# Reordering the attention part of the even layer, and swapping the roles of state and vectors in the sample delta rule

## The chip, the cores and the metric

The kernel runs on one core of a Trainium2 chip. TensorE (PE in the views; its weight loads are PEld) multiplies, VectorE (DVE) and ScalarE (ACT) work on SBUF and PSUM, GpSimd (POOL) does small work and starts some DMAs, SyncE (SP) starts the weight DMAs. The metric is the device time of one execution in microseconds. The kernel before took 1756.63 us as the median of three executions (1753.97 to 1757.15). Its profiled execution took 1756.62 us, of which 1754.9 us are the span from the first to the last instruction.

## The reference

Two trunk layers are run once, for a prompt of 256 tokens and for 8 sample sequences of one token each, D = 1024, all in float32. What the change touches is this, cut to what is computed:

```python
# layer 0, sample side of the differential attention (4 heads, two 64-wide halves, 256 past keys in two pages)
s1 = einsum(q1, k_all[..., :64]) * scale;  s2 = einsum(q2, k_all[..., 64:]) * scale
p  = softmax(s1) - lam * softmax(s2)
o  = p @ v_all
# layer 0, prompt side: the same with a causal mask over 256 keys, query blocks of 128
# layer 1, sample side of the gated delta rule, one token, per sequence b (8) and head h (8), S is 128 x 128
v_new = beta * (v - exp(g) * (k^T S))
o     = exp(g) * (q^T S) + (q . k) * v_new
S     = exp(g) * S + k v_new^T
```

The dense layers, the prompt's chunked delta rule and the experts' SwiGLU make up the rest; the change doesn't touch them.

## The kernel before, in words

Each engine has its own program, written out by hand, and the engines meet only through semaphores. `order(...)` lists the events of an engine in the order in which its one step semaphore counts them; `at(event, n)` is what another engine waits for. Every engine works strictly in the order of its program, so an instruction that waits holds up all that stands behind it on that engine.

The activations lie transposed (features on partitions, 264 token columns: 256 prompt, 8 sample). Dense layers split each weight piece into a high part (ACT, L551) and a low part (DVE, L554) and multiply three times. Weights come through a ring of three slots that SP fills ahead.

Even layer, attention. After the input projection PE sends each sample sequence's query row to all partitions (`query_rows`, L2180, two banks in turn); DVE multiplies it with the pages of past keys and sums (L1512, L1515), sequence by sequence, and each sum frees the bank for the query row after next (`k_used`) and a page buffer for POOL's next page load (`load_pages`, L741). Between the first two query rows and the third, PE transposes the keys (`ktok`, L2188), the tail of the convolution's input (L2191) and the last LRU states (`hlast`, L2195), and does three prompt score tiles (L2208, L2209). ACT copies the score tiles out (L1070), starts output DMAs (L1080 to L1088) and takes the exponentials (L1093). POOL masks four tiles at a time (L771), behind its page loads for sequences 6 and 7; DVE takes the row maxima after sequences 3 and 5 (`maxima`, L1502 to L1504). Then DVE forms the probabilities of the prompt heads (`mix_probs`, L1541; heads 0 and 1 first) and of the samples (L1546 to L1553, event `p_s`), PE transposes the samples' (L2229, L2230), DVE spreads them (L1557, L1559, event `pT_s`). Last, for each of four heads, PE transposes the prompt's probabilities (L2251), multiplies one sequence's value pages (`sample_values`, L2240) and the prompt's values (L2257 to L2259); ACT copies the transposed probabilities (`pT`, L1109) and then the result (`o_prompt`, L1111), head by head in that order. Sequences 4 to 7 and the norms (L2263, L2273) follow, then the output projection (L963).

Odd layer, sample delta rule. For head h `state_products` (L2491) loads each of the eight states as the weight (128x128) and moves two columns past it, the query and the key; `state_rows` (L2503) transposes the new value's three parts; `state_outer` (L2511) makes the outer product; `head_rows` (L2526) serves the prompt's norm for two heads in each of the iterations 2 to 5. PE's loop is: products of h+1, rows of h, outer of h-1, two head rows; ahead of the iteration 1 stand the prompt's sums of squares (`head_sums`, L2519, L2520). DVE's loop is: `sample_out` of h+1 (L1870 to L1880, after `s_ks` of h+1), `sample_outer_in` of h (L1890), `sample_state` of h-1 (L1897), and the prompt's norm (`normed`, L1909). ACT's loop is: wait for `s_ks` of h, scale the eight states of h (L1290), then wait for `sample_state` of h-1 and start the DMA that writes it out (L1310). Then comes the odd layer's output projection.

Of the kernel before, what the change touches and what calls it, by code (L numbers as in the profile page):

```python
# [14 lines left out]
P = 128  # L15
# [8 lines left out]
def program(nc, A, O):  # L24
# [6 lines left out]
    TT = TP // P  # L31
# [24 lines left out]
    with ExitStack() as ctx:  # L56
# [35 lines left out]
        def order(engine, *events):  # L92
            first = 0
            for name, count in events:
# [17 lines left out]
              ("qk_b", HB), ("qs_psum", 1), ("qk_b_keys", HB), ("qb_first", 2), ("ktok_psum", 3), ("tail_psum", 1),  # L112
              ("hlast_psum", 1), ("qb_rest", TS - 2), ("ss_psum", 1), ("self_psum", 1), ("pT_s_psum", 1),
# [6 lines left out]
              ("k_used_4", TS - 6), ("qk_self", 1), ("neg_max_s", 1), ("probs_first", 2), ("p_s", 1), ("probs_rest", HB - 2), ("pT_s", 1), ("ya_lo", 1),  # L120
# [9 lines left out]
        def qb_at(n):  # L130
            return at("qb_first", n) if n <= 2 else at("qb_rest", n - 2)
# [336 lines left out]
        qkv_s = cut(A_0 + HC * P + HC * R3 + 2 * R3, NQ, TS)  # L468
        q_s, k_s, v_s1 = (qkv_s[:, k * HC:(k + 1) * HC, :] for k in range(3))
# [536 lines left out]
        def _(act_e):  # L1006
# [277 lines left out]

            for h in range(HC + 1):
                if h < HC:
                    act_e.wait_ge(*at("s_egb", 1))
                    act_e.wait_ge(*at("s_ks", h + 1))
                    for b in range(TS):
                        last = SC.activation(s_all[h][:, b, :], s_all[h][:, b, :], ACT.Copy, scale=egb[:, 0, h, b:b + 1])  # L1290
                    last.then_inc(sig("s_scaled"), 1)
                if h == 1:
                    act_e.wait_ge(*at("on_ss", 1))
                    SC.activation(o_prompt_r, bank[0][0:HC, 0:TP], ACT.Sqrt, bias=eps_q[0:HC, :], scale=1.0 / DV).then_inc(sig("on_root"), 1)
                if h == HC - 2:
                    o_high(0)
                if h == HC - 1:
                    act_e.wait_ge(*at("s_o", HC))
                    SC.activation(o_sample_sq, oT[:, :, TP:T], ACT.Square).then_inc(sig("on_sample_sq"), 1)
                    act_e.wait_ge(*at("on_sample_ss", 1))  # L1300
                    SC.activation(o_sample_sq, bank[2][:, 0:HC * TS].rearrange("p (h b) -> p h b", h=HC), ACT.Sqrt, bias=eps_q[:], scale=1.0 / DV)\
                      .then_inc(sig("on_sample_root"), 1)
                    o_high(1)
                    act_e.wait_ge(*at("on_done", 1))
                    SC.activation(h_hi[:, :, TP:T], oT[:, :, TP:T], ACT.Copy).then_inc(sig("on_sample_hi"), 1)
                if not h:
                    continue
                h -= 1
                act_e.wait_ge(*at("s_state", h + 1))
                q.dma_start(O["delta_s_sample"][0, :, h].rearrange("b d e -> d b e"), s_all[h]).then_inc(sig(f"states{h // NLENT}_written"), 16)  # L1310
# [92 lines left out]
        def _(dve):  # L1403
# [150 lines left out]
            mix_probs(range(2, HB))  # L1554
# [4 lines left out]
            V.tensor_copy(pself, bank[6][:, NP_ * NB:(NP_ + 1) * NB]).then_inc(sig("pT_s"), 1)  # L1559
            dve.wait_ge(*at("pT_s", 1))  # L1560
# [288 lines left out]
            prod = inv[:, 0, 0:HC * TS].rearrange("p (h b) -> p h b", h=HC)  # L1849
            V.tensor_copy(q_s, qT[:, :, TP:T])  # L1850
            V.tensor_copy(v_s1, vT[:, :, TP:T])
            V.tensor_tensor(k_s, kT[:, :, TP:T], r_sample, ALU.mult).then_inc(sig("s_qkv"), 1)
            dve.wait_ge(*at("s_qkv", 1))
            V.tensor_tensor(prod, q_s, k_s, ALU.mult).then_inc(sig("s_prod"), 1)
# [8 lines left out]
            def sample_out(h):  # L1863
# [4 lines left out]
                qS = bank[2 + h % 2][:, 0:2 * TS].rearrange("p (b k) -> p b k", k=2)[:, :, 0]  # L1868
                kS = bank[2 + h % 2][:, 0:2 * TS].rearrange("p (b k) -> p b k", k=2)[:, :, 1]
# [10 lines left out]
                V.tensor_tensor(oT[:, h, TP:T], prod[:, 0, :], vn_t, ALU.add).then_inc(sig("s_o"), 1)  # L1880

# [205 lines left out]
        def _(pe):  # L2087
# [89 lines left out]
            def query_rows(b):  # L2177
                if b >= 2:
                    pe.wait_ge(*k_used_at(b - 1))
                PE.matmul(bank[4 + b % 2][:, 0:AW], ident[0:TS, b:b + 1].broadcast_to([TS, P]), qs_tok, start=True, stop=True)\  # L2180
                  .then_inc(sig("qb_first" if b < 2 else "qb_rest"), 1)
# [4 lines left out]
            for i, (t0, n) in enumerate(TOK):  # L2186
                for h in range(HB):
                    last = PE.transpose(bank[i][0:n, h * P:(h + 1) * P], proj[:, K_ + h, t0:t0 + n], ident[:])  # L2188
                last.then_inc(sig("ktok_psum"), 1)
            for t in range(NL):  # L2190
                last = PE.transpose(bank[7][0:TAIL, t * P:(t + 1) * P], proj[:, XR + t, T - TAIL:T], ident[:])  # L2191
# [21 lines left out]
            for b in range(2, TS):  # L2213
                query_rows(b)
                if b == 2:
                    prompt_scores(range(3, 5))
                if b == 3:
                    prompt_scores(range(5, HH))
# [7 lines left out]
            PE.matmul(bank[5][0:NB, 0:2], qk_s.rearrange("p h b -> p (h b)"), half2[:], start=True, stop=True).then_inc(sig("self_psum"), 1)  # L2226
            pe.wait_ge(*at("p_s", 1))
            for g in range(NP_):
                PE.transpose(bank[6][:, g * NB:(g + 1) * NB], ss[:, 0, g * P:(g + 1) * P], ident[0:NB, 0:NB])  # L2229
            PE.matmul(bank[6][:, NP_ * NB:(NP_ + 1) * NB], ss[:, 0, NP_ * P:NP_ * P + 1].broadcast_to([NB, P]), ident[0:NB, 0:NB],  # L2230
                      start=True, stop=True).then_inc(sig("pT_s_psum"), 1)
            pe.wait_ge(*at("pT_s", 1))
# [12 lines left out]
            for h in range(HB):  # L2245
                pe.wait_ge(*probs_at(h + 1))
                if h >= 2:
                    pe.wait_ge(*at("pT", h - 1))
                    pe.wait_ge(*at("o_prompt", h - 1))
                for c in range(3):  # L2250
                    last = PE.transpose(bank[h % 2][:, c * P:(c + 1) * P], sc_p[:, 2 * h, c * P:(c + 1) * P], ident[:])  # L2251
                last.then_inc(sig("pT_psum"), 1)
                sample_values(h)
                pe.wait_ge(*at("pT", h + 1))
                o = bank[2 + h % 2]
                v = [vtok[:, i, h * P:(h + 1) * P] for i in range(TT)]
                PE.matmul(o[:, 0:P], v[0], pT[h % 2][:, 0:P], start=True, stop=True)  # L2257
                PE.matmul(o[:, P:2 * P], v[0], pT[h % 2][:, P:2 * P], start=True, stop=False)
                PE.matmul(o[:, P:2 * P], v[1], pT[h % 2][:, 2 * P:3 * P], start=False, stop=True).then_inc(sig("pv_psum"), 1)  # L2259
# [224 lines left out]
            def state_products(h):  # L2484
# [3 lines left out]
                if h >= 2:  # L2488
                    pe.wait_ge(*at("s_o", h - 1))
                for b in range(TS):  # L2490
                    last = PE.matmul(bank[2 + h % 2][:, 2 * b:2 * b + 2], s_all[h][:, b, :],  # L2491
                                     qkv_s[:, h:h + HC + 1:HC, b], start=True, stop=True)
                last.then_inc(sig("s_ks"), 1)
# [35 lines left out]
            state_products(0)  # L2529
            for h in range(HC):  # L2530
                if h + 1 < HC:
                    state_products(h + 1)
                state_rows(h)
                if h:
# [222 lines left out]
```

## Time and profile before

| what | value |
|---|---|
| median of three executions | 1756.63 us |
| profiled execution | 1756.62 us |
| its span | 1754.9 us |
| PE, DVE, ACT, POOL busy | 95%, 76%, 61%, 11% of the span |
| mean granted clock of TensorE | 0.962 |
| chain that ended last | PE 84%, DVE 8%, ACT 3%, issue 2% |

The page's slices show where PE is not full: slice by slice (43.9 us each) PE is busy nine tenths or more nearly everywhere from slice 4 on, and the granted clock is 10 tenths or nearly, but for slices 1 to 3 (9, 9, 6 and 8 tenths in the first four) and slices 14 and 15 (7 and 5 tenths). These hold the even layer's attention and the odd layer's sample delta rule.

### The profile page before, as it was taken

Reading aid. Unit: us, or ns where it says so; the run is one execution under the profiler, and the core shown is the slowest. Engines: PE = TensorE matmul, PEld = TensorE weight load, DVE = VectorE, ACT = ScalarE, POOL = GpSimd, SP = SyncE. Lnnn points to the kernel's source line nnn. Section 1 sums busy time; section 2 is a strip of 40 time slices with the busy share of each in tenths; the row PEclk is TensorE's granted clock in tenths of the full one; section 3 lists DMA queues with packets and bytes.
Section 4 is the critical chain, followed back from the end, with each engine's and each line's share of the span. In section 5 each row is a group of like instructions: output and inputs, shape, how many; then the busy total and the mean of one; then the engine's idle time right before and its main releaser. Section 6 shows DMA issues by size and latency. Waiting matters only on the chain.

```text
span 1754.9 us, 25078 instructions
## 1 busy us (share of the span) xinstructions
PE 1675.1 (95%) x9513; PEld 1433.1 (82%) x9513; DVE 1328.7 (76%) x1443; ACT 1064.4 (61%) x1054; POOL 188.7 (11%) x234
## 2 busy tenths in 40 slices
PE   7979999999899988999999999999999999999996
PEld 7835999999879967888888888888888888888885
DVE  6883554556776745588898898888887998988985
ACT  5542543435752343677777777776776776776673
POOL 5020211003264601100000000000000000000000
PEclk9968999999999975999999999999999999999999
DMA  9542454653430026499899899899899899999992
GB/s 299 182 148 59 151 188 142 216 177 119 144 105 1 1 74 203 142 360 377 317 359 374 308 367 377 305 370 377 305 367 368 315 366 332 348 368 329 346 374 94
DMA packets 199194, 445.47 MB, mean 254 GB/s; under 512 B 9569, under 2 KB 20995, under 8 KB 199071
## 3 DMA queue, kind: packets, MB, share of 16 engines
q1 hardware_dynamic: 184698, 423.88, 67.1%
q0 software_dynamic: 3968, 12.85, 2.5%
q10 hardware_dynamic: 10448, 7.65, 1.5%
q8 instruction: 54, 0.88, 0.2%
q14 instruction: 26, 0.21, 0.0%
HBM read 437.28 MB, written 7.29 MB: 253 GB/s over the span
## 4 chain that ended last, share of the span: by engine, by line
PE 84%; DVE 8%; ACT 3%; issue 2%; PEld 2%; POOL 1%; DMA 0%; PEldq 0%; ACTq 0%; DVEq 0%; POOLq 0%
PE bank L2645 17%; PE bank L2624 12%; PE bank L2625 12%; PE bank L2629 12%; PE bank L963 5%; PE bank L967 5%; PE bank L976 5%; PE bank L2595 2%; DVE weight_lo L554 1%; ACT weight_hi L551 1%; PE bank L2425 1%; PE bank L2605 1%; PE bank L2491 1%; PE bank L2435 1%; PE bank L2438 1%
## 5 line engine op out<-in xcount | busy, mean ns | idle before, releaser
L554 DVE TENSOR_TENSOR weight_lo<-weight_ring,weight_hi 128x2048 fp32r<-128x2048 f32 (+1 forms) x352 | 797.2, 2274 | 234.3 <-ACT weight_hi L551 218.2
L551 ACT ACTIVATE weight_hi<-weight_ring 128x2048 fp32r<-128x2048 f32 (+1 forms) x358 | 680.2, 1903 | 304.6 <-PE bank L976 98.3
L2624 PE MATMUL bank<-weight_hi,h_lo 128*128 128x512 f32 x896 | 354.2, 395 | 0.1
L2625 PE MATMUL bank<-weight_hi,h_hi 128*128 128x512 f32 x896 | 349.2, 390 | 0.0
L2629 PE MATMUL bank<-weight_lo,h_hi 128*128 128x512 f32 x896 | 239.8, 389 | 0.0
L2629 PEld LDWEIGHTS bank<-weight_lo,h_hi 128*128 128x128 f32 x896 | 168.2, 188 | 35.0
L2624 PEld LDWEIGHTS bank<-weight_hi,h_lo 128*128 128x128 f32 x896 | 168.3, 188 | 34.6 <-DVE h_lo L1999 0.4
L2625 PEld LDWEIGHTS bank<-weight_hi,h_hi 128*128 128x128 f32 x896 | 168.4, 188 | 33.4
L2645 PE MATMUL bank<-weight_hi,h_lo 128*128 128x512 f32 x448 | 120.6, 391 | 1.8 <-DVE h_lo L2004 1.8
L2645 PE MATMUL bank<-weight_hi,h_hi 128*128 128x512 f32 x448 | 119.8, 389 | 0.0
L2645 PE MATMUL bank<-weight_lo,h_hi 128*128 128x512 f32 x448 | 119.8, 389 | 0.0
L554 DVE TENSOR_TENSOR weight_lo<-work,weight_hi 128x2048 fp32r<-128x2048 f32 x48 | 109.8, 2288 | 12.5 <-ACT weight_hi L551 12.5
L963 PE MATMUL bank<-n_hi,weight_hi 128*128 128x264 f32 x608 | 103.3, 292 | 8.9 <-issue 4.5
L551 ACT ACTIVATE weight_hi<-work 128x2048 fp32r<-128x2048 f32 x48 | 92.1, 1920 | 26.4 <-PE bank L2629 20.1
L967 PE MATMUL bank<-n_hi,weight_lo 128*128 128x264 f32 x608 | 100.6, 288 | 5.0 <-POOL weight_lo L607 5.0
L2645 PEld LDWEIGHTS bank<-weight_hi,h_lo 128*128 128x128 f32 x448 | 83.5, 188 | 19.0 <-DVE h_lo L2004 2.1
L2645 PEld LDWEIGHTS bank<-weight_hi,h_hi 128*128 128x128 f32 x448 | 84.1, 188 | 17.6
L2645 PEld LDWEIGHTS bank<-weight_lo,h_hi 128*128 128x128 f32 x448 | 84.1, 188 | 17.5
L963 PEld LDWEIGHTS bank<-n_hi,weight_hi 128*128 128x128 f32 x608 | 85.6, 192 | 13.4 <-issue 10.7
L963 PE MATMUL bank<-h_hi,weight_hi 128*128 128x264 f32 x464 | 87.6, 294 | 4.0 <-DVE work L1451 1.8
L967 PEld LDWEIGHTS bank<-n_hi,weight_lo 128*128 128x128 f32 x608 | 85.7, 192 | 5.4 <-POOL weight_lo L607 5.4
L967 PE MATMUL bank<-h_hi,weight_lo 128*128 128x264 f32 x464 | 85.4, 289 | 0.7 <-DVE weight_lo L554 0.7
(514 smaller groups left out, 2159.9 us busy)
## 6 DMA issues: line engine op xcount, KB each, us to landing
weight_ring<-in_moe_wg SPq DMA_DIRECT2D x104, 1024.0 KB, 7.2
weight_ring<-in_moe_wu SPq DMA_DIRECT2D x96, 1024.0 KB, 7.3
weight_ring<-in_moe_wd SPq DMA_DIRECT2D x88, 1024.0 KB, 6.6
work<-in_moe_wd SPq DMA_DIRECT2D x24, 1024.0 KB, 7.1
weight_ring<-in_w_in_o SPq DMA_DIRECT2D x8, 2048.0 KB, 8.6
work<-in_moe_wu SPq DMA_DIRECT2D x16, 1024.0 KB, 6.3
weight_ring<-in_ffn_wg SPq DMA_DIRECT2D x5, 2048.0 KB, 7.7
weight_ring<-in_ffn_wu SPq DMA_DIRECT2D x5, 2048.0 KB, 8.5
```

The lines of the kernel that those rows point to most:

```text
L551: return SC.activation(whi[:, p % SPLIT, 0:size], src, ACT.Copy).then_inc(sig("hi_done"), 1)
L554: V.tensor_tensor(wlo[:, p % SPLIT, 0:size], src, whi[:, p % SPLIT, 0:size].bitcast(F32), ALU.subtract)\
L963: PE.matmul(out, hi[:, jj, cols_], a_hi[:, j0 + j, :], start=first and j == 0, stop=False)
L967: PE.matmul(out, lo[:, jj, cols_], a_hi[:, j0 + part * half + jj, :], start=False, stop=False)
L976: last = PE.matmul(out, hi[:, jj, cols_], a_lo[:, j0 + j, :], start=False, stop=last_one and j == k - 1)
L2425: last = PE.matmul(bank[STREAM[u]][:, k * P:(k + 1) * P], Am[:, h, :], Tt[:, h, :], start=True, stop=True)
L2435: last = PE.matmul(bank[STREAM[u]][:, k * P:(k + 1) * P], Tm[:, h, :], Yb[:, h, :], start=True, stop=True)
L2595: last = PE.matmul(bank[(7, 3)[r]][:, jj * CAP:(jj + 1) * CAP], h_tok[:, i, j * P:(j + 1) * P], sel[:, i, :], start=i == 0, stop=i == NTT - 1)
L2624: PE.matmul(out, hte_l[:, j, :], hi[:, jj, :], start=j == 0, stop=False)
L2625: PE.matmul(out, hte_h[:, j, :], hi[:, jj, :], start=False, stop=False)
L2629: last = PE.matmul(out, hte_h[:, j, :], lo[:, jj, :], start=False, stop=j == KD - 1)
L2645: last = PE.matmul(bank[5 + hf][:, :], lhs[:, c % 2, k, :], rhs[:, kk, hf * CHUNK_COLS:(hf + 1) * CHUNK_COLS], start=c == 0 and k == 0 and ...
```

## The change

It has two parts, in two layers.

In the even layer the third query row (`qb_third`) is sent right after the key transposes, ahead of the tail, `hlast` and the first score tiles, and the later score tiles stand one query row later. PE transposes the probabilities of prompt heads 0 and 1 ahead of the wait for `p_s`, multiplies their values between the samples' transposes and the wait for `pT_s`, and then takes sample values and prompt heads 2 and 3 in turn. DVE spreads the samples' probabilities ahead of `mix_probs` of heads 2 and 3. ACT's program for this part is the same.

In the odd layer the weight of a product is now a 128x16 block that is zero but for two columns, the query and the key of one sequence, and the state (128x128) moves past it; the eight products of a head add up to 16 rows of 128 (queries, then keys) in the bank's columns 128 to 255. ACT copies these rows to SBUF (`take_rows`) and PE transposes them back to 16 columns (`state_columns`), which is now what `s_ks` signals. DVE writes the two columns of each block (`place_columns`).

```diff
-              ("qk_b", HB), ("qs_psum", 1), ("qk_b_keys", HB), ("qb_first", 2), ("ktok_psum", 3), ("tail_psum", 1),
-              ("hlast_psum", 1), ("qb_rest", TS - 2), ("ss_psum", 1), ("self_psum", 1), ("pT_s_psum", 1),
+              ("qk_b", HB), ("qs_psum", 1), ("qk_b_keys", HB), ("qb_first", 2), ("ktok_psum", 3), ("qb_third", 1), ("tail_psum", 1),
+              ("hlast_psum", 1), ("qb_rest", TS - 3), ("ss_psum", 1), ("self_psum", 1), ("pT_s_psum", 1),
...
# ACT, odd layer
+            def take_rows(h):
+                act_e.wait_ge(*at("s_rows", h + 1))
+                SC.activation(qk_rows[h % 2], bank[2 + h % 2][0:2 * TS, P:2 * P], ACT.Copy).then_inc(sig("s_rows_out"), 1)
+
+            take_rows(0)
             for h in range(HC + 1):
                 if h < HC:
                     act_e.wait_ge(*at("s_egb", 1))
-                    act_e.wait_ge(*at("s_ks", h + 1))
                     for b in range(TS):
                         last = SC.activation(s_all[h][:, b, :], s_all[h][:, b, :], ACT.Copy, scale=egb[:, 0, h, b:b + 1])
                     last.then_inc(sig("s_scaled"), 1)
+                if h + 1 < HC:
+                    take_rows(h + 1)
...
# DVE, even layer
-            mix_probs(range(2, HB))
             dve.wait_ge(*at("pT_s_psum", 1))
...
             V.tensor_copy(pself, bank[6][:, NP_ * NB:(NP_ + 1) * NB]).then_inc(sig("pT_s"), 1)
+            mix_probs(range(2, HB))
...
# DVE, odd layer
+            V.memset(qk_cols[0], 0.0)
+            V.memset(qk_cols[1], 0.0)
...
+            def place_columns(h):
+                step = 2 * TS + 1
+                V.tensor_copy(qk_cols[h % 2][:, 0:step * (TS - 1) + 1:step], q_s[:, h, :])
+                V.tensor_copy(qk_cols[h % 2][:, TS:TS + step * (TS - 1) + 1:step], k_s[:, h, :]).then_inc(sig("s_placed"), 1)
+
+            place_columns(0)
+            place_columns(1)
...
-                qS = bank[2 + h % 2][:, 0:2 * TS].rearrange("p (b k) -> p b k", k=2)[:, :, 0]
-                kS = bank[2 + h % 2][:, 0:2 * TS].rearrange("p (b k) -> p b k", k=2)[:, :, 1]
+                qS = bank[2 + h % 2][:, 0:TS]
+                kS = bank[2 + h % 2][:, TS:2 * TS]
...
                 V.tensor_tensor(oT[:, h, TP:T], prod[:, 0, :], vn_t, ALU.add).then_inc(sig("s_o"), 1)
+                if h + 2 < HC:
+                    place_columns(h + 2)
...
# PE, even layer
                 last.then_inc(sig("ktok_psum"), 1)
+            query_rows(2)
...
             prompt_scores(range(0, 3))
-            for b in range(2, TS):
+            for b in range(3, TS):
                 query_rows(b)
-                if b == 2:
+                if b == 3:
                     prompt_scores(range(3, 5))
-                if b == 3:
+                if b == 4:
                     prompt_scores(range(5, HH))
...
+            def prompt_probs(h):
+                pe.wait_ge(*probs_at(h + 1))
+                if h >= 2:
+                    pe.wait_ge(*at("pT", h - 1))
+                for c in range(3):
+                    last = PE.transpose(bank[h % 2][:, c * P:(c + 1) * P], sc_p[:, 2 * h, c * P:(c + 1) * P], ident[:])
+                last.then_inc(sig("pT_psum"), 1)
+
+            def prompt_values(h):
+                pe.wait_ge(*at("pT", h + 1))
+                if h >= 2:
+                    pe.wait_ge(*at("o_prompt", h - 1))
...
+            prompt_probs(0)
+            prompt_probs(1)
             pe.wait_ge(*at("p_s", 1))
...
+            prompt_values(0)
+            prompt_values(1)
             pe.wait_ge(*at("pT_s", 1))
...
+            sample_values(0)
+            prompt_probs(2)
+            sample_values(1)
+            prompt_values(2)
+            prompt_probs(3)
+            sample_values(2)
+            prompt_values(3)
+            sample_values(3)
...
# PE, odd layer
+                pe.wait_ge(*at("s_placed", h + 1))
                 for b in range(TS):
-                    last = PE.matmul(bank[2 + h % 2][:, 2 * b:2 * b + 2], s_all[h][:, b, :],
-                                     qkv_s[:, h:h + HC + 1:HC, b], start=True, stop=True)
-                last.then_inc(sig("s_ks"), 1)
+                    last = PE.matmul(bank[2 + h % 2][0:2 * TS, P:2 * P], qk_cols[h % 2][:, 2 * TS * b:2 * TS * (b + 1)], s_all[h][:, b, :],
+                                     start=b == 0, stop=b == TS - 1)
+                last.then_inc(sig("s_rows"), 1)
+
+            def state_columns(h):
+                pe.wait_ge(*at("s_rows_out", h + 1))
+                PE.transpose(bank[2 + h % 2][:, 0:2 * TS], qk_rows[h % 2], ident[0:2 * TS, 0:2 * TS]).then_inc(sig("s_ks"), 1)
...
             state_products(0)
+            state_columns(0)
             for h in range(HC):
                 if h + 1 < HC:
                     state_products(h + 1)
                 state_rows(h)
+                if h + 1 < HC:
+                    state_columns(h + 1)
                 if h:
                     state_outer(h - 1)
```

## Rows read from the trace of the kernel before

**Rows 1.** Windows: stretch, its us, busy of PE, PEld, DVE, ACT, POOL, clock, DMA.

```profile
624.00:690.00 66.00, 53.38 (x208) 39.45 (x209) 39.27 (x114) 29.13 (x78) 9.29 (x12) 0.57 0.51 164
...
642.00:644.00 2.00, 2.00 (x7) 0.62 (x5) 0.91 (x1) 1.98 (x5) 0.00 (x0) 0.58 0.00 0
```

**Rows 2.** Chain of waits, even layer's attention: start us, us, what.

```profile
104.62 0.43 PE bank L2208 x4
...
142.41 1.83 PE bank L2240 x4
...
145.11 0.33 PE bank L2251 x3
145.44 1.83 PE bank L2240 x4
```

**Rows 3.** Timeline, 100 to 129 us: start, us, engine, line, operation, idle before.

```profile
100.20 2.82 PE L2188 MATMUL bank<-ident,work 128*128 128x128 f32 x12
...
106.06 1.12 PE L2180 MATMUL bank<-work,ident 8*128 8x512 f32 x2
...
107.21 1.28 DVE L1512 TENSOR_TENSOR work<-work,bank 128x512 f32<-128x512 f32 x2 [1.61 <-PE bank L2180]
...
110.64 0.42 ACTq L1080 DMA_DIRECT2D out_k_prompt<-work  x1
...
111.01 0.54 POOL L741 DMA_DIRECT2D work<-in_cache_k  x1 [2.55 <-issue]
...
113.95 0.69 DVE L1502 TENSOR_REDUCE small<-work 128x4 f32<-128x512 f32 x1 [1.40 <-POOL work L771]
...
116.72 1.28 ACT L1093 ACT_TABLE_LOAD   x1 [5.49 <-issue]
...
123.20 0.40 ACT L1093 ACTIVATE work<-work,small 128x128 f32<-128x128 f32 x1 [1.57 <-DVE small L1504]
...
126.62 0.19 ACT L1093 ACTIVATION_READ_ACCUMULATOR work<-work,small 128x1 f32 x1
...
128.44 0.25 DVE L1527 RECIPROCAL small<-small 128x16 f32<-128x16 f32 x1
```

**Rows 4.** Timeline, 134 to 143 us, PE and ACT.

```profile
134.33 0.42 PE L2229 MATMUL bank<-ident,hT 32*128 32x32 f32 x2 [4.61 <-DVE hT L1553]
...
136.07 0.90 PE L2251 MATMUL bank<-ident,work 128*128 128x128 f32 x3 [0.89 <-DVE small L1559]
...
142.12 0.38 ACT L1111 ACTIVATE work<-bank 128x256 f32<-128x256 f32 x1 [4.62 <-PE bank L2259]
142.45 0.49 ACT L1109 ACTIVATE work<-bank 128x384 f32<-128x384 f32 x1
```

**Rows 5.** Chain of waits, sample delta rule and the output projection behind it.

```profile
633.80 6.62 PE bank L2491 x32
...
640.65 5.07 PE bank L2519 x16
...
646.24 1.89 PE bank L2491 x16
...
655.59 3.50 PE bank L2491 x16
...
692.12 0.88 PE bank L963 x4
```

**Rows 6.** Timeline, 650 to 683 us, DVE and ACT.

```profile
650.54 1.27 DVE L1897 TENSOR_TENSOR weight_ring<-weight_ring,bank 128x512 f32<-128x512 f32 x2
...
665.72 0.17 DVE L1870 TENSOR_TENSOR sm<-bank,sm 128x8 f32<-128x8 f32 x1 [1.95 <-PE bank L2491]
...
668.31 1.27 DVE L1897 TENSOR_TENSOR weight_ring<-weight_ring,bank 128x512 f32<-128x512 f32 x2
...
670.08 2.44 ACT L1290 ACTIVATE work<-work,sm 128x128 f32<-128x128 f32 x8 [4.14 <-DVE weight_ring L1897]
...
681.48 1.27 DVE L1897 TENSOR_TENSOR work<-work,bank 128x512 f32<-128x512 f32 x2
```

More of the change, by code:

```diff
@@ L119, in program @@
               ("q_done", 1), ("qk_done", 1), ("k_used_1", 1), ("lru_done", 1), ("k_used_2", 3), ("neg_max_1", 1), ("k_used_3", 2), ("neg_max_2", 1),
-              ("k_used_4", TS - 6), ("qk_self", 1), ("neg_max_s", 1), ("probs_first", 2), ("p_s", 1), ("probs_rest", HB - 2), ("pT_s", 1), ("ya_lo", 1),
+              ("k_used_4", TS - 6), ("qk_self", 1), ("neg_max_s", 1), ("probs_first", 2), ("p_s", 1), ("pT_s", 1), ("probs_rest", HB - 2), ("ya_lo", 1),
               ("o_inv", 1), ("mix_done", 1), ("mix_lo", 1), ("o_rows", 1), ("o_sample", 1), ("os_inv", 1), ("mix_done_s", 1), ("mix_lo_s", 1), ("norm1_inv", 1), ("ffn_act", NF), ("wba_lo", 1), ("dhist", 1),
@@ L130, in qb_at @@
         def qb_at(n):
-            return at("qb_first", n) if n <= 2 else at("qb_rest", n - 2)
+            return at("qb_first", n) if n <= 2 else at("qb_third", 1) if n == 3 else at("qb_rest", n - 3)
         K_USED = ((1, "k_used_1"), (4, "k_used_2"), (6, "k_used_3"), (TS, "k_used_4"))
@@ L468, in program @@
         qkv_s = cut(A_0 + HC * P + HC * R3 + 2 * R3, NQ, TS)
+        QK0 = A_0 + HC * P + HC * R3 + 2 * R3 + NQ * TS
+        qk_cols = [work[:, QK0 + k * 2 * TS * TS:QK0 + (k + 1) * 2 * TS * TS] for k in range(2)]
+        qk_rows = [work[0:2 * TS, QK0 + 4 * TS * TS + k * P:QK0 + 4 * TS * TS + (k + 1) * P] for k in range(2)]
+        assert QK0 + 4 * TS * TS + 2 * P <= A_0 + 4 * GRP
         q_s, k_s, v_s1 = (qkv_s[:, k * HC:(k + 1) * HC, :] for k in range(3))
@@ L2180, in query_rows @@
                 PE.matmul(bank[4 + b % 2][:, 0:AW], ident[0:TS, b:b + 1].broadcast_to([TS, P]), qs_tok, start=True, stop=True)\
-                  .then_inc(sig("qb_first" if b < 2 else "qb_rest"), 1)
+                  .then_inc(sig("qb_first" if b < 2 else "qb_third" if b == 2 else "qb_rest"), 1)
             for b in range(2):
@@ L2226, in _ @@
             PE.matmul(bank[5][0:NB, 0:2], qk_s.rearrange("p h b -> p (h b)"), half2[:], start=True, stop=True).then_inc(sig("self_psum"), 1)
+            def prompt_probs(h):
[9 more added lines that the diff above has]
+                    pe.wait_ge(*at("o_prompt", h - 1))
+                o = bank[2 + h % 2]
+                v = [vtok[:, i, h * P:(h + 1) * P] for i in range(TT)]
+                PE.matmul(o[:, 0:P], v[0], pT[h % 2][:, 0:P], start=True, stop=True)
+                PE.matmul(o[:, P:2 * P], v[0], pT[h % 2][:, P:2 * P], start=True, stop=False)
+                PE.matmul(o[:, P:2 * P], v[1], pT[h % 2][:, 2 * P:3 * P], start=False, stop=True).then_inc(sig("pv_psum"), 1)
+            prompt_probs(0)
+            prompt_probs(1)
             pe.wait_ge(*at("p_s", 1))
@@ L2242, in sample_values @@
                 last.then_inc(sig("v_pages_used"), 1)
[L2245 to L2259, printed above, removed]
+            sample_values(0)
[6 more added lines that the diff above has]
+            sample_values(3)
             def norm_sums(out, src, done):
```

## The prediction

> **What bounds the kernel now.** I read the page first: the chain that ended last is 84% PE, and its slices are full except around 44 to 175 us and 614 to 702 us, which are the two places that the change touches. The windows come next: in 624 to 690 us PE is busy 53.38 of 66 us at a mean granted clock of 0.57, nearly all of it at the lower level of 1.2 GHz; the clock rose while `head_sums` ran, in the stretch with 0.58 [rows 1]. Then the chain of waits in both places, and the timeline for what stands beside it. In the even layer the chain goes through DVE's page sums and maxima up to `p_s`, and from 136.07 us on through PE alone [rows 2 to 4]. In the odd layer's steady loop it is PE without a gap: 3.50 us of products per head and the work behind them [rows 5]; ACT and DVE wait there, ACT 4.14 us for DVE before each eight scalings [rows 6].
>
> The sum is made against the profiled execution's 1756.62 us (span 1754.9 us and 1.7 us around it), practically the median of 1756.63 us. Behind either place the chain runs on PE again, so what one place wins or loses passes to the end.
>
> **Even layer, the third query row.** DVE waited 1.61 us for it, until 107.21 us; the second sequence was done at 105.60 us [rows 3]. The key transposes end at 103.02 us, and a query row takes PE 1.12 us, at the lower clock twice that [rows 3]: the row is there by 105.3 us, and the 1.61 us go. What is late next: tail, `hlast` and scores come one query row later, an estimated 0.9 us since the transposes behind it then run at the clock that has risen meanwhile (bounds 0 and 2.2 us). The fourth sequence may then wait some tenths for its query row, but DVE stands behind POOL's mask for 1.40 us anyway [rows 3]; POOL starts the page load ahead of the mask 1.2 us after the third sequence (107.21 + 2.6 = 109.81, load at 111.01 us [rows 3]), so mask and maxima move up with it. ACT's output DMAs start when the last scores are out: 110.64 becomes about 111.5 us, and the table load at 116.72 us moves as much [rows 3]; but the second half of the exponentials waits 1.57 us for the maxima, which come 1.6 us earlier, and ends at 126.81 us where DVE needs it at 128.44 us [rows 3]. New: exponentials out at about 126.1 us, DVE there at 126.85 us. I take a gain of 1.6 us; if ACT's delay is 2.2 us, its end is 127.4 us and 1.0 us is left.
>
> **Even layer, prompt heads around the samples.** DVE's copies for `pT_s` come earlier, but PE doesn't wait there any more: its wait of 0.89 us at 136.07 us goes [rows 4]. The transposes of heads 0 and 1 move into PE's 4.61 us of idleness ahead of `p_s` [rows 4]: 0.90 and 0.33 us less behind it [rows 4, 2]. Sum 2.1 us. The values of heads 0 and 1 are only moved. But ACT's program still has `o_prompt` of head 0 ahead of `pT` of head 1, and PE no longer has sample values between: it ends the values of head 0, ACT copies 0.38 us, then 0.49 us, and only then can PE start head 1; from 142.09 to 142.94 us in the trace [rows 4], with two handovers 0.9 us of new idleness. Later heads have sample values of 1.83 us [rows 2] between, which hide the same pair of copies; the last page loads are needed some 9 us after their buffers come free. Gain 2.1 - 0.9 = 1.2 us. PE ran at the lower clock until 142 us; whether the earlier start lifts it sooner or the new gap later is not to be seen, and I bound it by -1.3 and +1.2 us, half of 2.5 us of work either way. Even layer: -1.6 - 1.2 = **-2.8 us**, bounds -4.1 and 0.
>
> **Odd layer, the products themselves.** A head is 16 passes either way (each float32 matmul is two). Before, a pass took 1.89 / 16 = 0.118 us at the full clock and 3.50 / 16 = 0.219 us at the lower [rows 5]. A pass that moves 128 float32 columns is seen in the scores: 0.43 / 4 = 0.107 us at the full clock [rows 2], so 0.213 us at half of it. The roles change, the price hardly: 0.2 us less per head. `place_columns` and the two memsets stand in DVE waits; in `sample_out` they add an estimated 0.2 us.
>
> The Trainium skill, "TensorE: Matmul & The Clock Gate", section "LDWEIGHTS (loading the stationary operand)", says that a load takes its number of columns over 1.2 ns, 13 ns for 16 columns where 128 take 107; and its section "Back-to-back issue gap" gives 134 cycles, 56 ns, for a matmul of 128 columns. By the two a pass would cost half of what I take. The trace's 0.107 us of a float32 pass speaks against that; what it would do is the third rival.
>
> **Odd layer, the ring.** The new chain runs through three engines. `sample_out` of h+2 waits for the columns of h+2, they for ACT's `take_rows` of h+2; in ACT's program that stands behind the scaling of h+1, and this behind the wait for `sample_state` of h-1, which on DVE stands behind `sample_out` of h+1. So one head follows the other by:
> - DVE, from `s_ks` to the end of `sample_state`: 665.72 to 668.31 + 1.27 = 669.58 us, 3.86 us [rows 6], and 0.2 us of `place_columns` in three of the five turns that count;
> - ACT, from there over the DMA start to the end of the scalings: 670.08 + 2.44 - 669.58 = 2.94 us [rows 6];
> - `take_rows`, 128 columns: 0.27 us, one step of 0.11 us below the 0.38 and 0.49 us of 256 and 384 columns [rows 4], bounds 0.1 and 0.38;
> - PE's small transpose with both handovers: 0.4 us, by two such in 0.42 us [rows 4], bounds 0.2 and 0.6.
>
> Together 7.47 us, bounds 7.1 and 7.8. PE's own work per turn, what it was and the transpose, fits in. Before, the five turns from the first `sample_state` (650.54 us) to the sixth (681.48 us) took 30.94 us [rows 6], 6.2 us each; now 5 x 7.47 + 0.6 = 37.95 us: **+7.0 us**, bounds +5.2 and +8.7.
>
> The start: products of head 0 from 633.8 to 637.2 us, rows, columns to 638.0; head 1 to 641.4 at the lower clock or 640.5 if it rises at 639.6; its rows and columns 0.7 us; `head_sums`, 5.07 us before [rows 5], 18 passes of 0.213 us at the full clock; products of head 2 1.7 us, rows and columns 0.65 us. The columns of head 2 are there at 647.4 or 649.2 us, and 2.7 us later the first `sample_state` starts: 650.1 or 651.9 us against 650.54. I take +0.5 us, bounds -0.4 and +2.5 (no rise at all). Behind the sixth `sample_state` nothing changes. Odd layer: **+7.5 us**.
>
> Sum: 1756.62 - 2.8 + 7.5 = **1761.3 us**, with own bounds 1757.5 and 1765.5.
>
> **The rivals.** First (0.15), nothing gained in the even layer, and a late start: ACT's bubble and a later rise of the clock eat the gain; -0.5 + 7.0 + 2.5 = +9: 1765.6 us. For it: the even layer's gains are of the size of a stall each. Against: two of the idle times that go are plain waits.
>
> Second (0.12), the clock, on the other side. If streaming the states lifts the clock for the whole stage and it stays up to the output projection, which begins at 0.88 us per four matmuls [rows 5], half of it at the full clock, some six groups cost 2.5 us less, the last outer products 0.9, the ring's PE steps 0.5 and the start 0.8: 4.7 - 4.7 = 0, 1756.6 us, not slower. It decides at the stretch between the last `sample_state` and the projection: the clock must be up there. For it: it rose under `head_sums`, whose weights have 8 columns [rows 1]. Against: in each turn PE would idle, and at the end it waits for DVE and ACT as before.
>
> Third (0.05), a half-price pass, as four matmuls of 264 columns in 0.88 us would suggest (0.107 us for 128 at the lower clock [rows 5]): the ring hides it but for the first three heads, 1.7 + 0.9 + 0.5 us: 1758.2 us.
>
> Fourth (0.10), a shorter ring: turns of 7.1 us and 4.1 us in the even layer: 1757.6 us.
>
> Fifth (0.08), the ring doesn't close and the change does what a shorter PE part promises: DVE's own 3.86 + 0.2 us per turn bound it; five turns 20.3 us, -10.6: 1756.62 - 10.6 + 0.5 - 2.8 = 1743.7 us. Against it stands the order of ACT's program.
>
> **How the numbers follow.** The forecast has 0.50, most of it between 1759 and 1764.5 us. A measurement of this kernel tells about 0.2% from no change, 3.5 us: 1753.1 and 1760.1 us. Slower: 0.45 of the forecast and the first rival, 0.60. Faster: the fifth and a little of the second, 0.09. The rest, 0.31, is no change. The range leaves out the fifth rival and the first's far end: 1755.8 to 1766 us.
>
> **What would show it.** In the even layer DVE no longer waits at its third sequence; PE starts sample values with about 0.9 us of idleness between the two value groups, and the output projection starts 2.8 us earlier. In the odd layer the chain of waits alternates DVE, ACT (scaling, `take_rows`) and PE's small transpose, the scalings start as soon as the DMA is issued, `sample_state` follows itself by 7.5 us, and PE waits for ACT in every turn. It would be wrong if turns were under 6.7 us (where the ring's loss only pays the even layer's gain), if a head's products took under 1.5 us at the full clock, or if the clock stayed up past 652 us into the projection.

## Result: slower by 0.3%, and the profile after

The changed kernel took 1762.38 us (median of 11 executions, 1759.97 to 1765.38), the kernel before 1756.99 us (11 executions beside it). The ratio is 1.0032, its 95% interval 1.0024 to 1.0041: slower, by 4.2 to 7.2 us. The forecast was 1761.3 us. It came out near the mark partly because two of its terms were wrong in opposite directions, as the experiments show.

The profiled execution took 1761.83 us, with a span of 1760.1 us and a mean granted clock of 0.966. First the odd layer. These windows of the changed kernel answer to [rows 1] (columns as there):

```profile
624.00:690.00 66.00, 43.68 (x209) 26.87 (x210) 36.84 (x123) 29.05 (x84) 9.28 (x12) 0.72 0.48 153
642.00:644.00 2.00, 2.00 (x12) 0.80 (x11) 0.15 (x1) 0.00 (x0) 0.00 (x0) 1.00 0.00 0
```

PE lost its place as the bound: it is busy 43.68 us where it had 53.38, with about the same number of matmuls and at a higher clock. The chain of waits of the changed kernel shows what took its place (start us, us, what; it answers to [rows 5]):

```profile
633.01 3.44 PE bank L2530 x16
...
639.51 3.55 PE bank L2562 x16
...
643.59 1.86 PE bank L2530 x16
...
648.66 1.21 DVE weight_ring L1919 x2
...
655.85 1.21 DVE weight_ring L1919 x2
657.08 0.38 ACTq L1320
657.51 2.44 ACT weight_ring L1298 x8
659.95 0.17 ACT work L1291
660.16 0.25 PE bank L2536
660.43 0.18 DVE sm L1890
...
661.68 0.06 DVE work L1869
661.75 0.17 DVE work L1870
661.92 1.11 DVE n_lo_odd L1912
663.03 1.21 DVE weight_ring L1919 x2
664.26 0.38 ACTq L1320
...
684.31 1.28 DVE work L1919 x2
...
691.94 1.25 PE bank L967 x4
```

From one `sample_state` (L1919) to the next the chain goes once around: ACT's DMA start, its eight scalings, its `take_rows` (L1291), PE's small transpose (L2536), and DVE's chain with `place_columns` (L1869, L1870) in it. The first `sample_state` starts at 648.66 us and the sixth at 684.31: 35.65 us for five turns, 7.13 us each, where the kernel before had 30.94 [rows 6]. Behind the sixth, 7.63 us pass until the output projection (L967), as before.

In the even layer DVE's, ACT's and POOL's timelines of the changed kernel answer to [rows 3] (start, us, engine, line, operation, idle before):

```profile
106.01 1.28 DVE L1522 TENSOR_TENSOR work<-work,bank 128x512 f32<-128x512 f32 x2
...
112.76 0.69 DVE L1512 TENSOR_REDUCE small<-work 128x4 f32<-128x512 f32 x1 [1.42 <-POOL work L775]
...
114.22 1.23 POOL L775 TENSOR_SCALAR_AFFINE_SELECT work<-work 128x512 f32<-128x512 f32 x2
...
114.61 0.87 DVE L1514 TENSOR_SCALAR small<-small 128x8 f32<-128x8 f32 x1
...
118.85 1.28 ACT L1097 ACT_TABLE_LOAD   x1 [5.99 <-issue]
...
127.93 0.25 DVE L1537 RECIPROCAL small<-small 128x16 f32<-128x16 f32 x1
```

The third sequence starts at 106.01 us without a wait. But the maxima that follow end in a scaling of 8 elements per partition (L1514) that takes 0.87 us, and the reciprocals start at 127.93 us, only 0.51 us earlier than before [rows 3]. Counted from the first page product (L1522, at 98.94 us here and L1512 at 98.66 us before) it is 0.8 us. Behind `p_s` the chain shows the gap between the two value groups (L2264 to L2266), made by ACT's copies L1115 and L1113:

```profile
133.82 0.42 PE bank L2272 x2
...
136.28 0.38 ACT work L1115
136.66 0.39 ACT work L1113
137.05 0.04 issue
137.10 0.79 PE bank L2264 x2
```

The even layer's output projection begins at 160.45 us, 1.39 us earlier than in the profile before (161.84), or 1.7 us counted from the first page product; the odd layer's at 691.94 instead of 689.12, 2.82 us later.

### The profile page after: what moved, and what is told of

Its sections match the earlier page's. It is cut to its first block, busy times and chain, and to the rows that moved or that the text cites. A ratio compares the mean times of both kernels' runs of the same rounds, so it can differ in the third digit from the quotient of the medians.

```text
span 1760.1 us, 25120 instructions
## 1 busy us (share of the span) xinstructions
PE 1672.3 (95%) x9521; PEld 1425.1 (81%) x9521; DVE 1331.6 (76%) x1461; ACT 1065.7 (61%) x1062; POOL 188.6 (11%) x234
## 4 chain that ended last, share of the span: by engine, by line
PE 82%; DVE 9%; ACT 4%; issue 2%; PEld 2%; POOL 1%; DMA 0%; PEldq 0%; ACTq 0%; DVEq 0%; POOLq 0%
PE bank L2691 17%; PE bank L2670 12%; PE bank L2675 12%; PE bank L2671 12%; PE bank L967 5%; PE bank L971 5%; PE bank L980 5%; PE bank L2641 2%; DVE weight_lo L558 1%; ACT weight_hi L555 1%; PE bank L2463 1%; PE bank L2651 1%; PE bank L2473 1%; PE bank L2476 1%; PE bank L2285 1%
## 5 line engine op out<-in xcount | busy, mean ns | idle before, releaser
L967 PE MATMUL bank<-n_hi,weight_hi 128*128 128x264 f32 x608 | 103.4, 292 | 8.9 <-issue 4.4
L555 ACT ACTIVATE weight_hi<-work 128x2048 fp32r<-128x2048 f32 x48 | 92.1, 1920 | 26.6 <-PE bank L2675 20.2
L967 PEld LDWEIGHTS bank<-n_hi,weight_hi 128*128 128x128 f32 x608 | 85.7, 192 | 13.4 <-issue 10.6
L967 PE MATMUL bank<-h_hi,weight_hi 128*128 128x264 f32 x464 | 87.6, 293 | 4.2 <-DVE work L1461 2.0
```

Source lines behind the costliest of these rows:

```text
L555: return SC.activation(whi[:, p % SPLIT, 0:size], src, ACT.Copy).then_inc(sig("hi_done"), 1)
L967: PE.matmul(out, hi[:, jj, cols_], a_hi[:, j0 + j, :], start=first and j == 0, stop=False)
```

## The experiments

Unless said otherwise each kernel was timed in five rounds, 12 executions, beside 35 (e1 to e4) or 29 (e5 to e8) of the kernel before, with medians of 1757.00 and 1757.70 us. A ratio is to that median, with its 95% interval in brackets.

**e1, the even layer's part alone.** The odd layer is that of the kernel before.

> The kernel before with the even layer's part alone. Theory (each part pays by itself, as the two traces show it): the output projection of the even layer starts 1.3 us earlier, the odd layer is that of before, the whole is 1 to 2 us faster than before, within what a measurement tells. Rival (the even layer's gain is not real, only where the profile of after happened to fall): projection at the same place within 0.3 us, whole time the same. In either case the small VectorE scaling behind the first maxima should again take some 0.9 us instead of 0.17 if it is POOL's second mask, now beside it, that holds it up.

Measured: 1757.09 us, ratio 0.9996 [0.9983, 1.0008]. The even layer's part is worth nothing on the whole. In its profile the even layer's projection starts at 163.06 us, 1.2 us later than before and not 1.3 us earlier; the small scaling takes 0.17 us and not 0.9; POOL's second mask runs behind it (from 116.53 us, the scaling ends at 115.82). Its 12 times fall in two groups, four from 1752.1 to 1754.0 us (mean clock 0.964) and eight from 1756.1 to 1760.2 us (0.960 to 0.962).

**e2, the odd layer's part alone.**

> The kernel before with the odd layer's part alone. Theory (the ring ACT, TensorE, VectorE): five turns between the first and the sixth state update of 35.5 us against 30.94, first update 1 us earlier, and the whole 3.5 to 5 us slower than before. Rival (the whole of the 5.4 us comes from the odd layer through TensorE's clock and not through the turns): turns as in the profile of after but the whole 5 to 8 us slower, with a mean clock that is lower than in the even-only kernel.

Measured: 1761.93 us, 1.0028 [1.0017, 1.0039], or +3.0 to +6.9 us: the loss is here. Five turns take 35.76 us (649.20 to 684.96) and the first state update comes 1.3 us earlier (24.36 us behind ACT's start of the prompt's state output, before 25.63), much as the theory had it; the mean clock of its profile is 0.966, not below e1's 0.961, so the rival fails. From ACT's start of the prompt's state output to the projection its profile has 67.76 us, the changed kernel's 67.81, the kernel before 64.21: +3.6 us. That place varies little: 67.71 to 67.81 in five profiles with the new products and the closed ring, 64.15 to 64.37 in the six of kernels with the old products.

**e3, the ring opened.** ACT takes rows two heads ahead, so that they no longer stand behind the scaling that waits for DVE.

```diff
             take_rows(0)
+            take_rows(1)
             for h in range(HC + 1):
...
                     last.then_inc(sig("s_scaled"), 1)
-                if h + 1 < HC:
-                    take_rows(h + 1)
...
+                if h + 2 < HC:
+                    take_rows(h + 2)
```

> After, with ACT copying the rows of head h+2 ahead of its wait for the state of head h-1, so that the copy stands behind neither that wait nor the scalings. Theory (the ring): five turns fall to between 25 us (VectorE's own work per turn, some 4.8 us, if the clock comes up) and 34.5 us (TensorE's own 6.9 us at the lower clock); the whole is 2 to 10 us faster than after. Rival (TensorE's streaming of the states is what makes a turn long): turns stay at 7.1 us, five at 35 us or more, and the whole stays where after is.

Measured: 1753.45 us, 0.9979 [0.9967, 0.9991], 8.9 us below the changed kernel by the medians. Five turns take 25.85 us, 5.17 each (first to sixth `sample_state`, 651.03 to 676.88 us). The same instructions in another order of ACT's program take 9.8 us off the five turns, so the ring was the bound. No single engine took the ring's place. In e3's chain of waits one turn, from 661.88 to 667.00 us, stays on DVE from one `sample_state` (L1920) to the next; ahead of it and behind it the chain goes through PE's products of a head (L2531) as well:

```profile
655.26 3.00 PE bank L2531 x16
...
661.88 1.20 DVE weight_ring L1920 x2
...
667.00 1.20 DVE weight_ring L1920 x2
...
670.24 3.15 PE bank L2531 x16
```

A stretch of POOL's timeline in e3 and DVE's beside it:

```profile
663.54 1.41 POOL L847 TENSOR_TENSOR hT<-hT,work 128x256 f32<-128x256 f32 x2 [3.92 <-DVE hT L1932]
```

```profile
661.81 1.27 DVE L1920 TENSOR_TENSOR weight_ring<-weight_ring,bank 128x512 f32<-128x512 f32 x2
663.00 0.85 DVE L1932 SCALAR_TENSOR_TENSOR hT<-hT,par,bank 128x256 f32<-128x256 f32 x2
663.78 0.15 DVE L1891 TENSOR_TENSOR sm<-bank,sm 128x8 f32<-128x8 f32 x1
663.96 0.33 DVE L1892 TENSOR_TENSOR sm<-work,sm 128x8 f32<-128x8 f32 x1
664.33 0.65 DVE L1893 TENSOR_TENSOR sm<-sm 128x8 f32<-128x8 f32 x1
```

A turn of DVE's holds what the prediction's fifth rival had left out: the prompt's norm for two heads (`normed`, L1932, 0.85 us), and small operations that end when POOL's products of the prompt's output with its gate (L847) do.

**e4, the gap between the values taken out.** ACT copies `pT` of heads 0 and 1 ahead of `o_prompt` of heads 0 and 1.

```diff
-            for h in range(HB):
+            def take_probs(h):
...
+            def take_values(h):
...
+            take_probs(0)
+            take_probs(1)
+            take_values(0)
+            take_values(1)
+            for h in range(2, HB):
```

> After, with ACT copying the transposed probabilities of heads 0 and 1 both ahead of the result of head 0. Theory: TensorE's 0.85 us of idleness between the values of heads 0 and 1 goes and the even layer's projection starts 0.8 us earlier than in after; the whole is up to 1 us faster. Rival (the gap only moved work that is late anyway, by the clock): projection within 0.3 us of after's place.

Measured: 1762.13 us, 1.0024 [1.0009, 1.0040]; by the medians nothing is gained over the changed kernel. In its profile the gap is gone, and from PE's first transpose behind `p_s` to the projection it is 24.4 us instead of 26.6. That is 2.2 us where 0.8 were expected, because the clock came back sooner too: at 136.2 us, 4.3 us behind `p_s`, and in the profile of after at 141.3 us, 7.5 us behind it. The first four sample values show it, in after and then in e4:

```profile
138.74 3.11 PE bank L2285 x4
```

```profile
135.70 2.10 PE bank L2295 x4
```

In the profiles of e5 and e6, which have no gap either, the clock is back 3.8 and 3.9 us behind `p_s`, in the other eleven 6.4 to 8.7 us. The times fall in two groups again: four from 1755.3 to 1756.9 us, eight from 1760.7 to 1765.5 us. Something in this stage varies by more than the gap is worth, which led to the next four.

**e5, both taken out** (the edits of e3 and e4 together).

> The changed kernel with both suspected losses taken out: ACT takes the rows of heads 0 and 1 ahead of its loop and those of h+2 just ahead of its wait for the state of h (as in e3), and the first two pT copies ahead of the first two o_prompt copies (as in e4). If the two losses are separate, e3's 8.9 us and the 2.2 us that e4's profile showed between p_s and the projection add up: about 1762.4 - 8.9 - 1.0 to 2.2 = 1751.3 to 1752.5 us, below the kernel before by 4.5 to 5.7 us. Rival: e4's median of 1762.13 us says that the gap between the values is worth nothing at the end; then it is e3's 1753.5 us.

Measured: 1751.44 us, 0.9970 [0.9958, 0.9982]. It is 2.0 us below e3 by the medians, but they are from two chips and the intervals overlap.

**e6, ACT's output DMAs behind the exponentials.** e5, and:

```diff
-            outs = (("ktok", 3, ktok, "k_prompt", "k_sample"), ("vtok", 3, vtok, "v_prompt", "v_sample"))
...
+            kv_out((("ktok", 3, ktok, "k_prompt", "k_sample"),))
             act_e.wait_ge(*at("ss_psum", 1))
...
             take_probs(1)
+            kv_out((("vtok", 3, vtok, "v_prompt", "v_sample"),))
+            lru_out()
```

> e5 with ACT's nine output DMAs moved from between the prompt scores and the exponentials to places behind them (two behind the prompt's exponentials, seven behind the first two pT copies). Theory: where PE's clock rises late in the even layer (about 109 us in the profiles of e1 and e3, 104 us in the others), the scores come late and the 6.0 us of DMA starts behind them put the exponentials on the chain: DVE waited 2.44 and 1.95 us for them there, 0 in the profile of after and e4. Moved, this wait goes in every profile: 0.8 to 2 us below e5's median, and a narrower spread. Rival: the exponentials hide either way, since DVE is bound by the page sums; then it is e5's time within 0.5 us, or above it by up to 1.5 us where the moved starts hold up the o_prompt copies.

Measured: 1749.21 us (6 executions), 0.9959 [0.9947, 0.9971]: 5.1 to 9.3 us faster than the kernel before, and the fastest of all. It is 2.2 us below e5 by the medians, but the intervals overlap. Its six times span 3.0 us, e5's twelve 8.0. ACT's first rows behind the scores in e6 show the exponentials waiting for DVE's maxima, no longer behind DMA starts:

```profile
110.84 0.49 ACT L1074 ACTIVATE work<-bank 128x384 f32<-128x384 f32 x1 [0.41 <-PE bank L2248]
111.35 1.28 ACT L1099 ACT_TABLE_LOAD   x1
113.98 0.40 ACT L1099 ACTIVATE work<-work,small 128x128 f32<-128x128 f32 x1 [1.35 <-DVE small L1530]
```

**e7, the third query row alone, and e8, the prompt heads alone** (the even layer's part cut in two, on the kernel before).

> The kernel before with the third query row moved ahead of the tail transposes and nothing else. The prediction's term: -1.6 us, 1755.4 us. Theory after e1: the row stands at the lower clock (2.07 us instead of 1.12) ahead of the scores, so ACT's starts and exponentials come 1 to 4 us later and take back the wait that DVE loses: between -1.5 us (clock up at 104 us) and +1 us (at 109 us), two groups of times some 3 us apart. DVE's wait of 1.61 us at its third sequence is gone in both.

> The kernel before with the prompt heads around the samples (transposes, values and DVE's order) and the query row where it was. The prediction's term: -1.2 us, 1755.8 us; p_s to projection 26.3 us, as in e1, where before had 27.5. If e1's nothing (1757.09 us) came from the query row alone, this one is 1 to 2 us faster than e1 and e7 is no faster than before; if it came from the heads, it is 1757 us and e7 is the faster.

Measured: e7 1758.68 us, 1.0009 [0.9998, 1.0020]; e8 1755.79 us, 0.9990 [0.9981, 1.0000]. Against 1757.70 us that is +1.0 us (-0.4 to +3.5) for the row and -1.9 us (-3.3 to 0) for the heads. By the times the heads give about what was forecast; the row gives nothing, or costs. e8 is below e1 and e7, the first of the two cases named. But e8's profile doesn't show the gain where it was expected: from PE's first transpose behind `p_s` to the projection it has 27.1 us, not 26.3, with the clock back 8.7 us behind `p_s`, where the kernel before has 27.5 and 7.7.

**r1 to r4, further profiles of the same kernels**, one execution each.

> The changed kernel once more, for a second profile. Theory: the even layer has two courses, set by when PE's clock rises behind the key transposes: at about 104 us, and then DVE doesn't wait for the exponentials and the first output projection starts 61.5 us after the first page product (as in the profile of after), or at about 109 us, and then DVE waits some 2 us for them and it is 63.5 us (as e1 and e3). One of the two is seen, and which one varies between runs of one kernel. Rival: the course belongs to the kernel; then this one is like the profile of after, 61.5 us. The last expert's last 24 matmuls take either 5.75 or 7.4 us, both of which have been seen without the change in the odd layer (e8, e7).

> As r1_after, a third profile of the changed kernel: 61.5 or 63.5 us from the first page product to the projection by the theory, 61.5 by the rival.

> The even layer's part alone once more. Its twelve times fell in two groups (1752.1 to 1754.0 us at a mean clock of 0.964, 1756.1 to 1760.2 us at 0.960 to 0.962) and its profile in the second. By the theory a profile in the first group shows the clock up at about 104 us or before and no wait of DVE for the exponentials; one in the second group repeats e1. By the rival it repeats e1 either way.

> The kernel before once more. Its clock was up at 104.2 us; by the theory the rise varies here too, and where it is at 109 us the third query row comes later than 107.21 us and DVE's wait of 1.61 us grows to 3 us and more. By the rival the profile is the one of before.

Measured: 1764.11, 1762.38, 1758.70 and 1758.89 us. From the first page product to the output projection r1 has 63.3 us and r2 63.2, the profile of after 61.5: the course does not belong to the kernel. The kernel before has 63.2 us in both of its profiles, so the late course gives nothing and the early one 1.7 us. Windows at the place where the clock rises, the changed kernel's first profile and then r1, the same program (columns as in [rows 1], the clock third from the end):

```profile
104.00:106.00 2.00, 2.00 (x16) 1.17 (x16) 1.84 (x3) 0.85 (x2) 0.41 (x1) 1.00 0.64 190
106.00:108.00 2.00, 2.00 (x10) 0.90 (x7) 1.95 (x4) 1.47 (x4) 0.54 (x1) 1.00 0.17 68
```

```profile
104.00:106.00 2.00, 2.00 (x4) 0.43 (x5) 1.97 (x4) 0.41 (x1) 0.54 (x1) 0.50 0.59 154
106.00:108.00 2.00, 2.00 (x12) 1.23 (x12) 1.83 (x4) 0.95 (x2) 0.44 (x1) 0.50 0.32 109
108.00:110.00 2.00, 2.00 (x13) 1.50 (x11) 1.10 (x2) 0.95 (x3) 0.64 (x2) 0.66 0.41 133
```

And what DVE then waits for in r1, the fourth sequence's query row and later the exponentials:

```profile
111.07 1.29 DVE L1522 TENSOR_TENSOR work<-work,bank 128x512 f32<-128x512 f32 x2 [1.97 <-PE bank L2202]
130.18 0.25 DVE L1537 RECIPROCAL small<-small 128x16 f32<-128x16 f32 x1 [1.79 <-ACT work L1097]
```

In r3 the clock didn't rise before 140 us at all (0.50 in the window from 94 to 140 us), and DVE waited 3.40 us for the fourth query row and 2.11 us for the exponentials. r4 repeats the profile of before up to its last microseconds, against what I expected of it: the clock up at 104 us, the third query row waited for 1.63 us. 0.50 is the lower of the clock's two levels, 1.2 GHz, and 1.00 the upper, 2.4 GHz. Over all profiles of this study the clock is up by 106 us in four of four without the row ahead of the scores, and in four of ten with it; in the other six it rises between 107 and 110 us or not before 140. Four against ten profiles don't show that the row makes a late rise more frequent, and the row can't be all of it: in four of the six late ones (e1, e3, e7, r1) the clock had already fallen at 92.3 to 92.6 us, ahead of everything that the row moves, and no profile without the row fell so early (93.9 to 94.9 us). Where the fall came 4.3 to 4.7 us ahead of the first page product, the clock rose 5.7 to 5.8 us behind that product in the three profiles without the row (before, r4, e2), and 9.4 and 46.5 us behind it in the two with it (r2, r3). These times are worked out from the granted clock of windows.

r4 also bears on a difference in the last expert that I had taken for the change's. Its last 24 matmuls, from the chain of waits of the kernel before (r4 first, then the profile of before), and of the changed kernel's first profile:

```profile
1734.75 7.38 PE bank L2645 x24
```

```profile
1733.23 5.75 PE bank L2645 x24
```

```profile
1737.40 7.41 PE bank L2691 x24
```

The kernel before shows either, so the slow end doesn't need the change. Over all profiles, however, the 24 matmuls take 7.35 to 7.41 us in all eight with the new products, and in those with the old ones 5.75 us in four (before, e1, e8, r3) and 7.38 in two (r4, e7). So many profiles make a link likely without showing it; how the new products, a thousand microseconds earlier, would bring it about stays open.

## Why the prediction came out as it did

**The ring: right in mechanism, a little too long.** The forecast had 7.47 us per turn, bounds 7.1 and 7.8; measured are 7.13. By the chain above, DVE takes 3.81 us with `place_columns` in it (660.43 to 664.24) and 3.67 without (681.92 to 685.59), forecast 3.86 + 0.2 and 3.86; ACT from there 2.89, forecast 2.94; `take_rows` 0.17 until PE is released, forecast 0.27; PE with handovers 0.31, forecast 0.4. Each part was a little below its term: a turn with `place_columns` takes 7.2 us, forecast 7.67, and one without 7.0 to 7.1, forecast 7.47. Five turns: +4.7 us instead of +7.0.

**The start: wrong in sign.** From ACT's start of the prompt's state output to the first `sample_state` it is 648.66 - 624.13 = 24.53 us, before 650.54 - 624.91 = 25.63: -1.1 us instead of +0.5. The price of a pass was right: head 0's 16 passes take 3.44 us and head 2's 1.86, at either level of the clock. The clock explains it: it was up early (0.98 in the window from 636 to 642 us, 0.50 before), so `head_sums` took 3.55 us instead of 5.07 [rows 5] and head 1's products ran at the full clock. The forecast had named both cases and gone between them; the better one came, and somewhat better than named.

**Behind the sixth state: right,** 7.63 us against 7.64. The clock fell back, and the projection's groups take 0.88 us as before, so the second rival fails at the point it named. The first rival's even layer without a gain came (e1), its late start did not. Of the fourth the ring's half held (7.13 us, where it had 7.1), and its 4.1 us from the even layer didn't come; turns are over 6.7 us, so the fifth fails; the third doesn't hold at 3.44 us a head. Odd layer: +3.6 us in the profiles, +4.9 by e2's medians, +7.5 forecast.

**The third query row: the term that failed.** The forecast let a wait of 1.61 us go and ACT's starts come 0.9 us later, "since the transposes behind it then run at the clock that has risen meanwhile". It took the time of the rise from one profile as fixed. With the row put ahead, most profiles have the clock still low there: the row takes 2 us, the fourth query row comes late (1.97 us of wait in r1), and scores, ACT's DMA starts and exponentials go back: the table load ahead of the exponentials starts 23.0 us behind the first page product in e1 and 25.1 in r3, before 18.1 (116.72 us in [rows 3], less 98.66). The bound of 2.2 us was too narrow for that. From the first page product to the reciprocals the kernel before takes 29.8 us; with the row it is 29.0 to 29.6 where the clock rises early (after, e4, e5, e6), 30.8 to 31.4 where it rises at 107 to 110 us, and 33.5 in r3: -0.8 to +3.7 us for a term of -1.6. Even in the early course 0.7 us or more of the gain is lost on DVE's scaling beside POOL's mask. A later rise may cost something without the row as well: e8, whose clock was up 7.6 us behind the first page product where before had 5.7, takes 30.7. By the times e7 puts the term at +1.0 us instead of -1.6. In e6, which takes the DMA starts away, the exponentials wait for the maxima alone; but its profile and e5's are of the early course, in which DVE doesn't wait for the exponentials with the starts in place either, so it isn't shown that the wait of the late course goes, nor, with six times against twelve, that the spread does.

**The prompt heads: right in the sum, one part open.** The idleness between the value groups was foreseen as 0.9 us, and is 0.38 + 0.39 and the handover, 136.28 to 137.10 us. Behind `p_s` six profiles with heads and gap have 26.2 to 26.7 us to the projection, four without the heads 27.5 to 27.6: 0.8 to 1.4 us, around the forecast's 1.2. e8's profile, with 27.2, has only 0.4 us of it, and its median is 1.9 us below (0 to 3.3). What the gap does to the clock, which the forecast could only bound, e4 shows: without it the clock is back some 3 us sooner.

So the even layer gave nothing (e1) where -2.8 us were forecast, the odd layer cost less than forecast, and the two errors cancelled: that the time came out within 1.1 us of the forecast is in good part luck. What remains open is one to two microseconds: by the profiles the stage of the odd layer costs +3.6 us, while the odd part alone costs +4.9 us and the whole +5.4 us by the medians (4.2 to 7.2). The last expert's slow end, 1.6 us and in all profiles with the new products, is of that size, but not shown to be the change's.

## What to carry to other kernels

When a result makes a detour through another engine, look at what stands ahead of the detour's instruction in that engine's program: here one copy behind a scaling that waits for DVE tied three engines into a ring, and moving that copy turned a loss of 5 us into a gain of 3.5. Where a stage runs across a change of the clock, one profile gives one of several courses; take the late rise as an equal case in the sum. Starts of output DMAs may be better placed behind the work that somebody waits for; here that was the fastest kernel, though not clear of the one without it.

## What the runs showed of the hardware

The same program gets its clock back at different times: in three profiles of the changed kernel it rose from 1.2 to 2.4 GHz in the window from 102 to 104 us, in that from 106 to 108, and in that from 108 to 110. It had fallen between 92 and 95 us in all three, and PE was busy all of the time from 94 us to the rise. In r3 PE was busy for all of the 20 us from 94 to 114 with the clock at 0.50 throughout.

Some small DVE operations end with the POOL operation beside them. The scaling L1514 takes 0.17 us in r1 and r2, and likewise in the profile of before, where the second mask runs later, but 0.87 us in the profile of after, from 114.61 to 115.48, where POOL's masks run until 115.45; in e5 it starts at 114.38 and takes 1.46 us, and the masks end at 115.81. In e3, L1893 takes 0.65 us and ends at 664.98 us, the second of POOL's two gate products (L847) at 664.95. Just ahead of it L1892 takes 0.33 us and ends at 664.29, the first of the two at 664.27. L1891, one of whose inputs is a PSUM bank, takes 0.15 us beside the first. In the chain of after, from 660.43 us on and with no POOL operation beside them, the same three (there L1890 to L1892) take 0.18 us each. Not every DVE operation is held up: in the profile of after the maxima L1513 take 1.21 us beside a mask, as in r1 without one.

The Trainium skill, "SBUF — State Buffer", section "Who interferes with whom", says that VectorE and GpSimd share a pair of ports under an exclusive lock, and that a VectorE instruction with two inputs from SBUF contends for it with a GpSimd instruction that reads SBUF, while one with at most one SBUF input outside the two-port modes does not. The trace agrees for L1891 to L1893 in e3, and with the lock in the other two places, where DVE ends within 0.03 us of POOL; L1514 has one SBUF input, and whether it runs in a two-port mode no run here shows.
